# 64-byte pads between the buffers that TensorE reads in a two-block transformer forward pass

## The reference

```python
z = xn @ w_in[l] + b_in[l]                       # first block, and y @ w_out
h = h + swiglu(rmsnorm(h, g_ffn[l]), w_gate[l], w_up[l], w_down[l])
proj = x @ w_in                                  # second block: q, k, v, then @ w_out
u = x @ w_in                                     # FFN in, 1024 -> 2 * 2816
return (jax.nn.silu(g) * val) @ w_out            # FFN out ("down"), 2816 -> 1024
```

## Time and profile before

| | us |
|---|---|
| median of 3 runs | 1815.69 |
| lowest, highest | 1814.77, 1815.97 |
| span of the profiled execution, first to last instruction | 1818.9 |
| TensorE busy in it | 1774.2 |
| weight loads (PEld) busy | 1477.6 |
| GpSimd busy | 1029.9 |
| ScalarE busy | 795.8 |
| VectorE busy | 765.2 |

### The profile page before, as it was taken

One profiled execution on the slowest core, in us unless ns is written; L12 is line 12 of the kernel. 1 busy time (PEld: TensorE's weight loads), 2 busy tenths in 40 slices (PEclk: granted clock), 3 DMA queues, 4 the chain that ended last, 5 costly groups with the idle time before them and its releaser, 6 DMA issues.

```text
span 1818.9 us, 26859 instructions
## 1 busy us (share of the span) xinstructions
PE 1774.2 (98%) x8755; PEld 1477.6 (81%) x8755; DVE 765.2 (42%) x1382; ACT 795.8 (44%) x1674; POOL 1029.9 (57%) x926
## 2 busy tenths in 40 slices
PE   8999999999999999999999999999999999999997
PEld 6879888888887888788888888877777888888886
DVE  7963000001235556553333322487875533333224
ACT  5644323322245555464444422555565644444231
POOL 7856555555462333466666655555554666666551
PEclk9999999999999999999999999999999999999999
DMA  5312333323334454323333233333332233332332
GB/s 153 92 47 82 104 92 92 101 87 103 91 90 115 123 133 122 86 73 99 102 92 94 85 104 87 82 94 81 87 77 79 63 111 93 96 100 78 104 91 97
DMA packets 327253, 171.94 MB, mean 95 GB/s; under 512 B 43459, under 2 KB 316949, under 8 KB 327189
## 3 DMA queue, kind: packets, MB, share of 16 engines
q1 hardware_dynamic: 327172, 171.12, 33.8%
q10 hardware_dynamic: 16, 0.00, 0.0%
HBM read 152.15 MB, written 2.10 MB: 85 GB/s over the span
## 4 chain that ended last, share of the span: by engine, by line
PE 87%; DVE 5%; POOL 3%; ACT 2%; issue 1%; DMA 1%; SPq 0%; DVEq 0%; ACTq 0%; POOLq 0%
PE bank L982 24%; PE bank L984 24%; PE bank L983 24%; PE attended L982 2%; PE attended L983 2%; PE attended L984 2%; PE turned L1423 1%; POOL WL L741 1%; PE attended L1439 1%; PE bank L1055 1%; PE bank L1067 1%; POOL psums L804 1%; PE bank L1068 1%; DVE small L2453 0%; PE score L1406 0%
## 5 line engine op out<-in xcount | busy, mean ns | idle before, releaser
L741 POOL TENSOR_TENSOR WL<-raw,WH 128x512 fp32r<-128x512 f32 (+3 forms) x656 | 774.8, 1203 | 555.6 <-ACT WH L1604 553.1
L982 PE MATMUL bank<-XL,WH 128*128 128x512 f32 x1432 | 568.8, 397 | 3.7 <-DVE work L2576 1.2
L984 PE MATMUL bank<-XH,WL 128*128 128x512 f32 x1432 | 557.8, 390 | 0.0
L983 PE MATMUL bank<-XH,WH 128*128 128x512 f32 x1432 | 557.4, 389 | 0.0
L1604 ACT ACTIVATE WH<-raw 128x512 fp32r<-128x512 f32 (+3 forms) x656 | 338.5, 565 | 307.7 <-PE bank L984 190.9
L984 PEld LDWEIGHTS bank<-XH,WL 128*128 128x128 f32 x1432 | 269.7, 188 | 56.8
L982 PEld LDWEIGHTS bank<-XL,WH 128*128 128x128 f32 x1432 | 270.1, 189 | 55.6 <-DVE work L2576 1.5
L983 PEld LDWEIGHTS bank<-XH,WH 128*128 128x128 f32 x1432 | 270.4, 189 | 49.9
L982 PE MATMUL bank<-HL,WH 128*128 128x512 f32 (+1 forms) x528 | 200.6, 380 | 0.0
L983 PE MATMUL bank<-HH,WH 128*128 128x512 f32 (+1 forms) x528 | 200.3, 379 | 0.0
L984 PE MATMUL bank<-HH,WL 128*128 128x512 f32 (+1 forms) x528 | 200.3, 379 | 0.0
(11 more groups left out here) (366 smaller groups left out, 2532.0 us busy)
## 6 DMA issues: line engine op xcount, KB each, us to landing
raw<-in_ffn_w_in SPq DMA_DIRECT2D x88, 512.0 KB, 3.8
raw<-in_w_gate SPq DMA_DIRECT2D x22, 512.0 KB, 3.8
raw<-in_w_up SPq DMA_DIRECT2D x22, 512.0 KB, 3.9
raw<-in_ffn_w_out SPq DMA_DIRECT2D x28, 384.0 KB, 3.3
raw<-in_ffn_w_out SPq DMA_DIRECT2D x28, 320.0 KB, 3.2
raw<-in_a_w_in SPq DMA_DIRECT2D x16, 512.0 KB, 4.2
raw<-in_kv_w SPq DMA_DIRECT2D x32, 256.0 KB, 3.2
raw<-in_w_in SPq DMA_DIRECT2D x12, 512.0 KB, 3.8
```

The source lines that it names most:

```text
L741: pool.tensor_tensor(wl, x, wh, ALU.subtract).then_inc(w_lo, 1)
L982: pe.matmul(out_, wh, xl, start=start, stop=False)
L983: pe.matmul(out_, wh, xh, start=False, stop=False)
L984: return pe.matmul(out_, wl, xh, start=False, stop=stop)
```

## The change

Pads of 16 float32 (64 bytes a partition) are added to the layout: `stagger_x` between `XH` and `XL`, `stagger_raw` ahead of `raw`, `stagger_w` between `WH` and `WL`, `stagger_parts` ahead of the area that the stages share, and `stagger_h` between `HH` and `HL`. No instruction is added, removed or moved. (`XL` now ends 64 bytes past `last_rows`, which the second pad covers.)

```diff
         XH = sb("XH", [P, DT, S], F32R, stack=wide)
+        sb("stagger_x", [P, 16], stack=wide)
         XL = sb("XL", [P, DT, S], F32R, stack=wide)
         wide.close()
         yout = sb("yout", [P, 2 * QT, S])
         last_rows = sb("last_rows", [P, DT, S])
+        sb("stagger_raw", [P, 16])
         raw = sb("raw", [P, RAW, DT, P])
         WH = sb("WH", [P, SLOTS, DT, P], F32R)
+        sb("stagger_w", [P, 16])
         WL = sb("WL", [P, SLOTS, DT, P], F32R)
...
+        sb("stagger_parts", [P, 16])
         first = ExitStack()
...
         HH = sb("HH", [P, FT, S], F32R, stack=ffn)
+        sb("stagger_h", [P, 16], stack=ffn)
         HL = sb("HL", [P, FT, S], F32R, stack=ffn)
```

## The result

The changed kernel takes 1837.88 us (4 runs, 1836.61 to 1841.90) against 1815.83 (4 runs) for the one before: 1.0123 times as long, 95% interval 1.0110 to 1.0135. That is 22 us slower, where 22 us faster was forecast. The time lies 3 us above the stated range.

What follows compares the result with a forecast made beforehand. TensorE's matmul-to-matmul gap was taken as the bound. Whole rows gaining 7.5, 12.3 and 3.1 us, with half rows +1.3, -1.8, -0.4, gave 22.0 gained: 1815.69 to 1793.7, forecast 1794 us, range 1765 to 1835, likeliest case 1786 to 1802.

Steps and rivals of the forecast that it cites:

- What bounds the kernel: Dense stages: TensorE closed, so only the gap from one matmul to the next sets the time; no other engine near.
- The reading of the gaps: All dense stages: gap is row length plus few 16-cycle units; whole X 32 + 2, H 32 + 3, halves 16 + 2, 16 + 1.
- I take 33 for a different pair: Whole rows: a pair with unlike residues between equal ones takes 33 units, 220.0 ns; the step trusted least, 35 the rival.
- the two "equal" ones: X's pairs whose moving rows and next weights share a residue modulo 128 after the change, put at 34 units each.
- The term for X: Whole rows of X: 34, 34, 33 units, mean 224.4 ns, 3390 x 2.2 = 7.5 us gained.
- The term for H: Whole rows of H: from 233.3 to 224.4 ns, 1386 x 8.9 = 12.3 us gained.
- The term for O: Whole rows of O: 33, 34, 33 units, 233.3 to 222.2 ns, 282 x 11.1 = 3.1 us gained.
- The half rows: 256-token rows: equal pairs 18 units, different 17; X 1.3 us gained, H 1.8 and O 0.4 lost.
- The residues: Addresses modulo 128 of one matmul's moving rows and the next one's weights; equal gave even units, different odd.
- The rival that never settles: Gate, up, in and q/k/v stages: mixed residues keep all whole rows at 231.7 ns, 16.5 to 22 us lost; chance 0.20.
- Its three groups of rows: Evidence for never settling: forget gates 232.1 ns, X after transposes 232 for five gaps, value products 233 over three.
- The rule that spoke against it: Matmul weight loads: two independent read ports, so loading next weights steals no read bandwidth; the change would do nothing.

Runs made afterwards that it cites:

- the ladder: Whole computation left out; 36 to 72 back-to-back matmuls on constants, repeating one address pair or triple: X's triple 226.7 ns before, 232.6 after; H's 233.3 both.
- the sweep: Second ladder kernel, computation left out: distance between moving rows and weights swept from 0 to 1024 bytes; whole rows 226.7 ns at 0 and 256, up to 236.7.

## Why the prediction was wrong

**What bounds the kernel**: right. Only TensorE's gaps moved, TensorE stayed closed in the dense stages, and no other engine mattered. The reading of the gaps as the row's length and a number of 16-cycle units was right for the pure runs of the trace before, with the same numbers in the ladder; at other distances only the sum of a cycle is a whole number of units. That addresses set the levels was right, and measured by itself.

**The step that failed** is "I take 33 for a different pair", and ahead of it the idea that a gap belongs to a pair of matmuls. No gap of 33 units showed as a steady level anywhere: 34 is the least of whole rows, in the sweep too. In the trace after, a run of X repeats only after nine gaps, and the two "equal" ones don't keep their 34 units: the gaps of pairs cannot be added up. Its mean is 34.89 units, 232.6 ns, where the forecast had 34, 34 and 33, 224.4. The term for X was put at 7.5 us gained and measured 22 lost. Its count was low too: 3390 rows, with those of the attention units left out, where 4181 gaps of X run uninterrupted. The term for H was put at 12.3 gained and measured 0.2: H left one uniform level of 35 units for a mix that averages 35. The term for O, 3.1, measured 0.6. The half rows were put at 0.9 lost together and measured 1.8.

**The residues** were taken modulo 128, since the trace of before could not tell more: there X had a distance of 0 and H and O of 192 modulo 256. By 256 the distances after, to the next matmul's weights, are (0, 128, 192) for X and (128, 0, 64) for H, so that even "two equal pairs of three" was one.

**The rows that had it.** The rival that never settles was put at 0.20, at 1832 to 1837 and 231.7 ns; measured 1837.88 and 232.6. That so near a number came out is in part luck, for mixed runs do settle: the ladder's repeat a cycle within ten gaps, at a mean of 231.1 to 234.4 by the mix, and the rival took 231.7 for all of them. H's mix settled at 233.3, where the rival had it gain 2.2 us. Its three groups of rows were the ones that I had read in which distances or streams mixed, and all were at 232 to 233. I discounted them as short or narrow. The ladder shows that 16 columns of weights at a fixed distance run at 231.7 too, so the earlier trace rows were indeed no proof by themselves. The earlier trace rows came nearest: X out of step costs 232 until it falls into its gap of 226.7, and none of the long runs of X does so after the change. The half rows, on which I leaned instead, follow another order: the best distance of one is nearly the worst of the other.

**The rule that spoke against it.** The whole rows of the two ladder kernels differ by up to 10.0 ns (226.7 to 236.7) with only TensorE at work and nothing but an address changed. The Trainium skill, in "TensorE: Matmul & The Clock Gate", section "Step-by-step: what each phase is for", has the weight load leaving the running matmul's read bandwidth alone. By that rule the change would have done nothing. That these gaps come from the two reads meeting is argued from the dependence on their distance, not shown; a load of 16 weight columns in place of 128 leaves whole rows at 231.7, with the weights at the rows' address and 64 past it alike, which a simple collision of reads would not lead one to expect.

**What stays open**: which mechanism gives 34 units at distance zero and 35 at 192, why half rows invert the order, and why some distances have two steady cycles. Nothing here looks inside.

## What to carry to other kernels

Where TensorE has no idle time and every matmul brings new weights (here float32r, the only type tried), lay out all moving and stationary buffers at one common distance modulo 256 bytes, zero for rows of 512: it costs a pad and gained 0.3% here. Pads that make distances differ among successive matmuls lose against that layout even when two pairs of three keep the good distance: such mixes ran at 231.1 and 232.0 against 226.7. Before you price a mix by rows of pure runs, look in the trace for any stretch where things mix, however short, or run the mix alone as a ladder of some fifty matmuls: it gave the levels of X and H in both kernels to 0.1 ns. Take its mean over whole cycles.

## What the runs showed of the hardware that was not expected

- The gap of float32r matmuls with fresh weights depends on the distance of moving rows to weights modulo 256 bytes: 226.7 ns at 0, 228.9 at 64, 232.4 or 233.3 at 128, 233.3 at 192, 236.7 at 4.
- Such a stream settles into an exactly repeating cycle of gaps, of 1 matmul at distance 0, 3 at 64, 7 or 2 at 128, 9 in the mix of X after, 15 in one other mix. A cycle's sum is a whole number of units of 16 cycles.
- For rows of 256 the order turns over: 120.0 at 0, 118.7 at 128, 113.3 at 192. At 64 two levels were seen, 117.8 and 113.3, by what ran before. Rows of 384 gave 173.3 at 0 and at 64.
- A weight load of 16 columns in place of 128, at distance 0, does not make the gap shorter: 231.7 against 226.7. With 64 columns it is 230.0.
- After a change of distance a run of whole rows needs up to ten gaps to settle, at 224 to 240 ns each.
